# Forgetting attention: both heads' scores block by block in two banks, q and k as fp32r high and low parts, one transpose bank

## What is computed

```python
kvf = rmsnorm(x, kv_norm_g) @ kvf_w
k = kvf[..., :D].reshape(B, S, FOX_HEADS, FOX_HEAD_DIM)
v = kvf[..., D:2 * D].reshape(B, S, FOX_HEADS, FOX_HEAD_DIM)
log_f = jax.nn.log_sigmoid((kvf[..., 2 * D:] + fgate_b).astype(jnp.float32))
c_bhs = jnp.cumsum(log_f, axis=1).transpose(0, 2, 1)

def fox_attention(h, w_q, w_o, k, v, c_bhs):
    ...
    q = (h @ w_q).reshape(B, nb, Q_BLOCK, FOX_HEADS, FOX_HEAD_DIM).transpose(1, 0, 2, 3, 4)
    ...
    def block(args):
        qi, ci, i = args
        s = jnp.einsum("bqhd,bkhd->bhqk", qi, k).astype(jnp.float32) * scale
        s = s + (ci[..., :, None] - c_bhs[:, :, None, :])
        q_pos = i * Q_BLOCK + jnp.arange(Q_BLOCK)
        mask = key_pos[None, :] <= q_pos[:, None]
        s = jnp.where(mask[None, None], s, -jnp.inf)
        p = jax.nn.softmax(s, axis=-1)
        return jnp.einsum("bhqk,bkhd->bqhd", p.astype(v.dtype), v)
```

## Time and profile before

| | |
|---|---|
| device time, median of 3 runs | 2522.62 us (2521.87 to 2522.66) |
| span of the profiled execution | 2519.9 us |
| PE busy | 2420.8 us, 96% |
| DVE, ACT, POOL busy | 54%, 36%, 10% |
| DMA | 202.29 MB, mean 80 GB/s |

### The profile page before, as it was taken

One profiled execution on the slowest core, in us unless ns is written; L12 is line 12 of the kernel. 1 busy time (PEld: TensorE's weight loads), 2 busy tenths in 40 slices (PEclk: granted clock), 3 DMA queues, 4 the chain that ended last, 5 costly groups with the idle time before them and its releaser, 6 DMA issues.

```text
span 2519.9 us, 34043 instructions
## 1 busy us (share of the span) xinstructions
PE 2420.8 (96%) x11130; PEld 1905.2 (76%) x11130; DVE 1349.5 (54%) x1893; ACT 901.2 (36%) x1395; POOL 249.5 (10%) x234
## 2 busy tenths in 40 slices
PE   6999999999999899988999999999999999999997
PEld 4776667888888677764878888877777687888886
DVE  4444665644444659996546445464444445544544
ACT  3444444453233443334333222244333333322222
POOL 3001110201010300001112000030000202100003
PEclk9999999999999999998999999999999999999999
DMA  4111212333333233330213333322111121333332
GB/s 122 46 47 43 59 50 83 92 115 94 100 92 95 80 105 104 100 100 25 78 48 95 97 100 96 96 85 76 50 42 50 50 75 58 93 96 99 98 92 84
DMA packets 394553, 202.29 MB, mean 80 GB/s; under 512 B 13626, under 2 KB 392683, under 8 KB 394474
## 3 DMA queue, kind: packets, MB, share of 16 engines
q1 hardware_dynamic: 393136, 198.56, 26.8%
q0 software_dynamic: 1008, 2.62, 0.3%
q10 hardware_dynamic: 330, 0.08, 0.0%
HBM read 199.11 MB, written 2.10 MB: 80 GB/s over the span
## 4 chain that ended last, share of the span: by engine, by line
PE 85%; DVE 5%; issue 4%; ACT 3%; DVEq 2%; ACTq 1%; POOLq 0%; DMA 0%; POOL 0%; SPq 0%
PE bank L1591 23%; PE bank L1593 23%; PE bank L1592 23%; PE bank L1575 3%; PE bank L1935 2%; PE bank L2079 2%; DVE m_w_lo L966 2%; PE bank L2104 1%; PE bank L2000 1%; PE bank L1976 1%; PE bank L1710 1%; PE bank L1686 1%; PE bank L1722 1%; PE bank L1724 1%; PE bank L2080 1%
## 5 line engine op out<-in xcount | busy, mean ns | idle before, releaser
L491 ACT ACTIVATE m_w_hi<-m_raw 128x1024 fp32r<-128x1024 f32 x373 | 395.1, 1059 | 1054.7 <-PE bank L1593 1048.0
L1591 PE MATMUL bank<-m_h_hi,m_w_hi 128*128 128x512 f32 x1504 | 618.1, 411 | 9.1 <-DVE m_h_lo L1005 5.3
L1593 PE MATMUL bank<-m_h_hi,m_w_lo 128*128 128x512 f32 x1504 | 588.4, 391 | 0.0
L1592 PE MATMUL bank<-m_h_lo,m_w_hi 128*128 128x512 f32 x1504 | 587.5, 391 | 0.0
L966 DVE TENSOR_TENSOR m_w_lo<-m_raw,m_w_hi 128x1024 fp32r<-128x1024 f32 x373 | 512.1, 1373 | 94.0 <-ACT m_w_hi L491 91.9
L1591 PEld LDWEIGHTS bank<-m_h_hi,m_w_hi 128*128 128x128 f32 x1504 | 283.5, 188 | 81.9 <-issue 24.8
L1593 PEld LDWEIGHTS bank<-m_h_hi,m_w_lo 128*128 128x128 f32 x1504 | 283.0, 188 | 60.6
L1592 PEld LDWEIGHTS bank<-m_h_lo,m_w_hi 128*128 128x128 f32 x1504 | 283.7, 189 | 56.5 <-issue 5.4
L1591 PE MATMUL bank<-m_f_hi,m_w_hi 128*128 128x512 f32 x688 | 270.1, 393 | 6.2 <-DVE m_w_lo L966 6.1
L1593 PE MATMUL bank<-m_f_hi,m_w_lo 128*128 128x512 f32 x688 | 268.0, 389 | 0.0
L1592 PE MATMUL bank<-m_f_lo,m_w_hi 128*128 128x512 f32 x688 | 267.8, 389 | 0.0
(11 more groups left out here) (338 smaller groups left out, 3372.1 us busy)
## 6 DMA issues: line engine op xcount, KB each, us to landing
m_raw<-in_ff_w SPq DMA_DIRECT2D x256, 256.0 KB, 3.0
m_raw<-in_w_in SPq DMA_DIRECT2D x48, 256.0 KB, 3.1
m_raw<-in_conv_pw_w SPq DMA_DIRECT2D x48, 256.0 KB, 2.9
m_raw<-in_w_ffn_gate SPq DMA_DIRECT2D x44, 256.0 KB, 3.1
m_raw<-in_w_ffn_up SPq DMA_DIRECT2D x44, 256.0 KB, 3.2
m_raw<-in_w_ffn_down SPq DMA_DIRECT2D x40, 256.0 KB, 2.8
m_raw<-in_w_gate SPq DMA_DIRECT2D x32, 256.0 KB, 2.9
m_raw<-in_mem_wk SPq DMA_DIRECT2D x32, 256.0 KB, 2.9
```

The costliest lines, as they stand in the source:

```text
L491: act.activation(WH[:, v % 2], RAW[:, v % 2], ACT.Copy).then_inc(s.w_hi, 1)
L1591: pe.matmul(o, WH[:, r, k, :], hi, start=start, stop=False)
L1592: pe.matmul(o, WH[:, r, k, :], lo, start=False, stop=False)
L1593: last = pe.matmul(o, WL[:, r, k, :], hi, start=False, stop=stop)
```

## The change

The scores are made block by block for both heads at once. `sc(b)` replaces `sc(x)`: it stands at the hooks -0.5, 1.5, 3.5 and 5.5 and writes head 0 into one bank and head 1 into the next, over all four banks `SBK`. The pieces x now run block by block, x=2b+e; `tr(x)` and `av(x)` keep their hooks. All transposes of probabilities go to `TR`, so `tr(x)` waits for the copy `pt(x-1)` rather than `pt(x-2)`.

The product of queries and keys becomes three fp32r matmuls with 64 rows for each head (high times high, low times high, high times low), with the heads alternating. The parts are made from `FQN` and `FKN`: the high parts by ACT (`fox_split`, two copies of 128x512 at the start of its third list), the low parts by DVE (two subtractions in place of two copies). ACT now waits for the keys' evacuation, and DVE for ACT.

```diff
+        FQH, FQL, FKH, FKL = (at(f"fox_{n}", 72 + 2 * i, [P, T], F32R) for i, n in
+                              enumerate(["q_hi", "q_lo", "k_hi", "k_lo"]))
...
+                def fox_split(p):
+
+                    def f():
+                        act.wait_ge(s.fx_staged, p * 3 + 2)
+                        if not isinstance(p, int) or p > 0:
+                            act.wait_ge(s.fx_s, p * 8)
+                        act.activation(FQH[:], FQN[:], ACT.Copy).then_inc(s.fx_hi, 1)
+                        act.activation(FKH[:], FKN[:], ACT.Copy).then_inc(s.fx_hi, 1)
+                    return f
...
                     return [fox_high(prev) + [ex(0), turned_v(FV, s.fx_vt, s.fx_v, p), ex(1), pt(0), ex(2), pt(1), ex(3)],
                             [pt(2), ex(4), pt(3), ex(5), pt(4), ex(6), pt(5)],
-                            [ex(7), pt(6), pt(7)]]
+                            ([fox_split(p + 1)] if more else []) + [ex(7), pt(6), pt(7)]]
...
                 def fox_current(p):
-                    return current(FQN, FKN, FQ, FK, s.fx_staged, s.fx_s, 8, s.fx_cur, p)
+
+                    def f():
+                        for i, (full, hi, lo) in enumerate(((FQN, FQH, FQL), (FKN, FKH, FKL))):
+                            dve.wait_ge(s.fx_hi, p * 2 + (i + 1))
+                            dve.tensor_tensor(lo[:], full[:], hi[:].bitcast(F32), ALU.subtract).then_inc(s.fx_cur, 1)
+                    return f
...
-                    def sc(x):
+                    def sc(b):
                         def f():
-                            e, b = x // 4, x % 4
-                            w, r = (b + 1) * P, 64 * e
-                            bank = SBK[x % 3]
+                            w = (b + 1) * P
+                            banks = [SBK[(2 * b + e) % 4] for e in range(2)]
                             pe.wait_ge(s.fx_cur, p * 2 + 2)
-                            if x >= 3:
-                                pe.wait_ge(s.fx_exp, p * 8 + (x - 2))
-                            pe.matmul(bank[:, 0:w], FQ[r:r + 64, b * P:w], FK[r:r + 64, 0:w], start=True, stop=False)
-                            pe.matmul(bank[:, 0:w], pick(SEL, p * 2 + e), CP[:, 0:w], start=False, stop=False)
-                            pe.matmul(bank[:, b * P:w], IDENTB, NEG_CAUSAL, start=False, stop=True)\
-                                .then_inc(s.fx_s, 1)
+                            if b >= 2:
+                                pe.wait_ge(s.fx_exp, p * 8 + 2 * b - 2)
+                            for q, k, first in ((FQH, FKH, True), (FQL, FKH, False), (FQH, FKL, False)):
+                                for e in range(2):
+                                    r = 64 * e
+                                    pe.matmul(banks[e][:, 0:w], q[r:r + 64, b * P:w], k[r:r + 64, 0:w], start=first,
+                                              stop=False)
+                            for e in range(2):
+                                pe.matmul(banks[e][:, 0:w], pick(SEL, p * 2 + e), CP[:, 0:w], start=False, stop=False)
+                            for e in range(2):
+                                pe.matmul(banks[e][:, b * P:w], IDENTB, NEG_CAUSAL, start=False, stop=True)\
+                                    .then_inc(s.fx_s, 1)
...
-                            if x >= 2:
-                                pe.wait_ge(s.fx_pt, p * 8 + (x - 1))
-                            for j in range(x % 4 + 1):
-                                last = turn((TR, SBK[3])[x % 2][:, j * P:(j + 1) * P], FP[:, x % 2, j * P:(j + 1) * P])
+                            if x >= 1:
+                                pe.wait_ge(s.fx_pt, p * 8 + x)
+                            for j in range(x // 2 + 1):
+                                last = turn(TR[:, j * P:(j + 1) * P], FP[:, x % 2, j * P:(j + 1) * P])
...
-                    events = [(FOX_STEP * x + start, i, make(x)) for x in range(8)
-                              for i, (start, make) in enumerate(((-0.5, sc), (FOX_TR, tr), (FOX_AV, av)))]
+                    events = [(FOX_STEP * 2 * b - 0.5, 0, sc(b)) for b in range(QB)]
+                    events += [(FOX_STEP * x + start, 1 + i, make(x)) for x in range(8)
+                               for i, (start, make) in enumerate(((FOX_TR, tr), (FOX_AV, av)))]
```

More of the change, by code:

```diff
@@ L916, in fox_high, with fox_pieces @@
                     return [] if p is None else [oh]
-                def fox_pieces(p, prev):
+                def fox_split(p):
[6 more added lines that the diff above has]
+                    return f
+                def fox_pieces(p, prev, more=True):
                     def ex(x):
                         def f():
-                            w = (x % 4 + 1) * P
+                            w = (x // 2 + 1) * P
                             act.wait_ge(s.fx_nm, p * 8 + (x + 1))
-                            act.activation(FP[:, x % 2, 0:w], SBK[x % 3][:, 0:w], ACT.Exp, bias=ST[:, x:x + 1],
+                            act.activation(FP[:, x % 2, 0:w], SBK[x % 4][:, 0:w], ACT.Exp, bias=ST[:, x:x + 1],
                                            accum_out=ST[:, 8 + x:9 + x]).then_inc(s.fx_exp, 1)
@@ L928, in f @@
                         def f():
-                            w = (x % 4 + 1) * P
+                            w = (x // 2 + 1) * P
                             act.wait_ge(s.fx_tr, p * 8 + (x + 1))
-                            act.activation(FPT[:, x % 2, 0:w], (TR, SBK[3])[x % 2][:, 0:w], ACT.Copy).then_inc(s.fx_pt, 1)
+                            act.activation(FPT[:, x % 2, 0:w], TR[:, 0:w], ACT.Copy).then_inc(s.fx_pt, 1)
                         return f
@@ L935, in fox_pieces @@
                             [pt(2), ex(4), pt(3), ex(5), pt(4), ex(6), pt(5)],
-                            [ex(7), pt(6), pt(7)]]
-                group([None] * 3, None)
+                            ([fox_split(p + 1)] if more else []) + [ex(7), pt(6), pt(7)]]
+                group([None] * 3, [[], [], [fox_split(0)]])
                 group([None] * 3, fox_pieces(0, None))
@@ L942, in _ @@
                         group([None] * 3, fox_pieces(i * 2 + (1 + j), i * 2 + j))
-                for part in fox_pieces(FOX_PAIRS - 1, FOX_PAIRS - 2) + [fox_high(FOX_PAIRS - 1)]:
+                for part in fox_pieces(FOX_PAIRS - 1, FOX_PAIRS - 2, False) + [fox_high(FOX_PAIRS - 1)]:
                     for f in part:
@@ L1523, in f @@
                         def f():
-                            w = (x % 4 + 1) * P
+                            w = (x // 2 + 1) * P
                             dve.wait_ge(s.fx_s, p * 8 + (x + 1))
-                            dve.reduce_max(ST[:, 16 + x:17 + x], SBK[x % 3][:, 0:w], AX.X)
+                            dve.reduce_max(ST[:, 16 + x:17 + x], SBK[x % 4][:, 0:w], AX.X)
                             dve.drain()
@@ L1537, in on @@
                         for x in range(8):
-                            e, b = x // 4, x % 4
+                            e, b = x % 2, x // 2
                             last = dve.tensor_scalar(FON[:, b, 64 * e:64 * e + 64],
```

## The result

| | before | after |
|---|---|---|
| median of 4 runs | 2522.64 us (2521.87 to 2524.19) | 2490.4 us (2488.6 to 2491.96) |
| ratio | | 0.9875, interval 0.9863 to 0.9887 |
| span of the profiled execution | 2519.9 us | 2488.1 us |

The change makes the kernel 32.2 us faster, where 23.5 was forecast. A run is 1.9 to 2.0 us longer than its span (2490.0 for 2488.1, 2521.87 for 2519.9), not 2.7 as I had taken it.

The account below looks back on a forecast made before the run. PE's instructions were taken to bound the stage: scores 8.18 to 5.32 us a pair, plus 0.08 for a restart, gain 2.94, 23.5 for eight pairs; span 2496.4, median 2499.1 us, range 2492 to 2510.

Parts of the forecast that it names:

- What bounds the stage: In the stretch changed, PE's instructions set the time: PE is busy throughout a middle pair of 32.62 us.
- The scores before: Old score visits on PE: 7.38 us a pair for both heads, plus 0.80 for entering, 8.18 in sum.
- The fixed parts after: New score visits on PE: entering 0.40, fixed cost 0.84 and bf16 matmuls 1.46, together 2.70 us a pair.
- The fixed 0.21 a visit: Each score visit on PE pays 0.21 us for entering with an unhidden weight load and leaving; 0.84 a pair.
- The 24 fp32r matmuls: 64-row score matmuls on PE: heads' streams overlap, loads follow 0.107 us apart; 2.62 us a pair, bounded by 1.91 and 3.85.
- the rival in which the loads overlap as well: Weight loads of both heads overlap: 1.91 us for the 24 matmuls, 2493.4 us in all; chance 0.15.
- The sign that I had named: In PE's timeline, first fp32r score matmul to first bf16 one takes 0.85 us for every width up to 384.
- The dropped visit: The visit at hook 0.5 disappears, and with it one slow restart of a unit's slice on PE: 0.08 us a pair.
- ACT's cover: ACT's high parts delay pt(6), but tr(7) is due 0.33 us after it may start, so the work stays hidden.
- DVE: Two subtractions replace two copies on DVE: 0.54 us more, ahead of 4.01 us of idle time; nothing moves.
- No overlap of the heads: Rival: the heads' matmuls run one after the other, 3.85 us for the 24, 2508.9 us in all; chance 0.15.
- exposed loads at each change: Rival: each change of array half exposes its weight load, 7.4 us for the 24, 2537.3 us in all; chance 0.08.

Follow-up runs that it names:

- the second execution of the change: The changed kernel unaltered, profiled again on another chip; the two repeats took 2491.96 and 2492.54 us.
- the run with the extra copies: The changed kernel with two more ACT copies of 128x512 to a scratch tile ahead of the two high parts; 2496.58 us, ratio 0.9899.
- the mask between the heads: The changed kernel with head 0's fp32r, bf16 and mask matmuls all ahead of head 1's in each visit; 2515.79 us, ratio 0.9981.
- one head in a visit: The kernel before with only the split into fp32r high and low parts, keeping eight visits a pair; 2515.63 us, ratio 0.9979.

## Why the prediction was off

**What bounds the stage: right.** It is PE's instructions. In the middle pairs after, there is no idle time of PE; the one wait in them that the trace names (`L2101 <- issue`, 0.16 us) is a missing record.

**The scores before: right.** Added up row by row, the eight distances are 7.45 us, against 7.38 with 384 columns by interpolation and both heads taken as alike.

**The fixed parts after: right.** With four entries at 0.10 and the visits' 0.69, 0.89, 1.18 and 1.45 us, the scores take 4.61 us a pair. Of the 4.21 in the visits, 2.66 lie ahead of the bf16 matmuls by the second execution of the change (0.48, 0.55, 0.72, 0.90; in the first, a bf16 record is missing in the visits of 512 columns), and 1.55 behind, where I had 1.46. The fixed 0.21 a visit, 0.84 in all, isn't measured by itself; the rows of 256 columns, with 0.22, 0.12 and 0.21 us from start to start, fit it.

**The 24 fp32r matmuls: the step that failed.** I took 2.62 us, "the loads all come over one path, and the trace shows them 0.107 apart there". Measured: 2.66 less the fixed 0.84 is 1.82 us, against 1.91 by the rival in which the loads overlap too, to which I had given 0.15. The sign that I had named, 0.85 us to the first bf16 matmul for every width up to 384 columns, is 0.48, 0.55 and 0.72. The two loads that are 0.107 apart in the earlier trace rows belong to one float32 matmul of one half, and I carried their distance over to loads of different halves, where no row spoke. The term was 0.80 too large, 6.4 us in eight pairs. That is three quarters of the miss in the span, 2496.4 - 2488.1 = 8.3 us. To it come 0.07 a pair from the sum of before (0.6 us) and the 1.9 us ahead of the stage, less 0.09 a pair for the bf16 part (0.7 us): 8.2. Without the 1.9 us of chance the median would have been about 2492.3 us, 6.8 off and just inside the range of 2492 to 2510; the mechanism would have been as wrong. As a median the miss is 8.7, since I had put 2.7 us around the span where the runs show 1.9 to 2.0.

**The dropped visit: right in kind.** The sum with it, 7.45 + 0.80 - 4.61 + 0.08 = 3.72, meets the measured 3.74.

**ACT's cover: right.** PE goes on at `tr(7)` without idle time, and the rows that answer are

```profile
1771.98 0.67 ACT L935 ACTIVATE m_fox_p<-bank,m_stats 128x512 f32<-128x512 f32 x1
...
1772.64 0.58 ACT L943 ACTIVATE m_fox_pt<-bank 128x512 f32<-128x512 f32 x1
...
1773.64 0.60 PE L1592 MATMUL bank<-m_con,m_fox_p 128*128 128x128 f32 x4
```

`pt(6)` is done at 1773.22, 0.42 us ahead of `tr(7)`. I had 0.33; with 0.15 us from ACT's end to PE's start, as in the run with the extra copies, 0.27 of it can be used.

**DVE: right.** The two low parts take 0.68 and 0.69 us, and the idle time behind them is still 4.48 us, which answers the earlier trace rows:

```profile
1778.09 1.05 DVE L1556 TENSOR_SCALAR m_fox_o<-bank,m_stats 128x64 f32<-128x64 f32 x5 [4.48 <-PE bank L2126]
```

**The other rivals.** No overlap of the heads (30.9 us a pair) and exposed loads at each change (34.5) are refuted by the timeline; the mask between the heads (31.92) shows what no overlap costs.

## What to carry over

Where two matmuls of 64 rows lie on different halves of the array and write different banks, put them next to each other with no full-row matmul in between: the second then costs next to nothing, in fp32r and in float32, and the order in which the two halves' matmuls are written hardly matters (tried in fp32r). Move the masks and the other full-row matmuls behind both. Different banks are what all these kernels have; one bank for both was not tried. Before doing it, see whether PE is what the stage waits for: with PE busy all through, 30 us came off the span, and in a stage where PE already waited for DVE, 9 us of saved PE time came back as waits, with a lower clock beside them.

## What was not expected of the hardware

- The two halves don't hold to the written order between them: with head 0's three fp32r matmuls written first, head 1's start together with them (records x2 at 1758.17, 1758.39 and 1758.51 us).
- Weight loads of the two halves overlap fully (two in 0.19 us), while loads of one half follow each other 0.10 to 0.12 us apart.
- A float32 matmul of 64 rows, which leaves two records, overlaps with that of the other half as well: four records, 0.64 us for 256 columns, as for one head.
- A 64-row matmul starts 0.15 us behind the start of a mask matmul (1761.98 to 1762.13, masks in between), where a full-row matmul starts 0.03 behind it (1757.69 to 1757.72, one head in a visit).
